# A two-block transformer step on one core: the unit-matrix products that fill TensorE's waits are left out

## What is computed

```
for l in range(2):                                   # first block
    mod = silu(c) @ w_ada[l] + b_ada[l]              # shift, scale, gate, twice
    h = rms_norm(x, norm1_g[l]) * (1 + scale1) + shift1
    proj = h @ w_in[l]
    mix = concat(mla_group(proj...), conv_group(proj...)) @ w_out[l]
    x = x + gate1 * mix
    h2 = rms_norm(x, norm2_g[l]) * (1 + scale2) + shift2
    x = x + gate2 * expert_choice_ffn(h2, w_router[l], w_gate[l], w_up[l], w_down[l])
xn = rms_norm(x, mix_norm_w)                         # second block
q, f, i, g, lru_x, lru_gate = split(xn @ w_in_2)
x = x + concat(hgrn2_mix(q, f, i, g), rglru_mix(lru_x, lru_gate)) @ w_out_2
x = x + (silu(gate) * up) @ w_down_2                 # gate, up = split(rms_norm(x) @ w_gate_up)
out = rms_norm(x)
```

## Time and profile before

| | us |
|---|---|
| median of 3 runs | 3365.02 |
| lowest, highest | 3361.22, 3365.70 |
| profiled execution, device time | 3364.91 |
| its span, first to last instruction | 3363.1 |
| outside the span | 1.8 |

### The profile page before, as it was taken

How to read it: one execution, slowest core, us unless ns; L and a number is a source line. 1 busy time by engine, 2 the same in 40 slices (tenths; PEclk the granted TensorE clock), 3 DMA queues, 4 the chain that set the end, 5 groups by cost and what they waited for, 6 DMA issues and landing times. The chain is left out here.

```text
span 3363.1 us, 43670 instructions
## 1 busy us (share of the span) xinstructions
PE 3237.5 (96%) x15480; PEld 2605.3 (77%) x15480; DVE 2704.8 (80%) x2483; ACT 1784.7 (53%) x1912; POOL 685.3 (20%) x550
## 2 busy tenths in 40 slices
PE   7999997999999999999799999999999999999998
PEld 4859884888888786897588888878777878888786
DVE  7988886888888798888788888886744488888767
ACT  4254534888888534444378888863333353333223
POOL 0212100111111020320011111104453023233233
PEclk9999998999999999999899999999999999999999
DMA  5130167999999412005599999962110434444953
GB/s 200 38 97 13 33 211 281 398 400 389 400 389 399 172 46 90 21 10 177 193 363 391 402 388 403 391 255 98 47 38 13 150 107 162 138 156 148 379 238 137
DMA packets 143518, 703.07 MB, mean 209 GB/s; under 512 B 19376, under 2 KB 28080, under 8 KB 90672
## 3 DMA queue, kind: packets, MB, share of 16 engines
q1 hardware_dynamic: 132240, 664.65, 51.4%
q0 software_dynamic: 8928, 32.51, 3.6%
q10 hardware_dynamic: 2240, 4.46, 0.3%
HBM read 608.75 MB, written 85.46 MB: 206 GB/s over the span
## 5 line engine op out<-in xcount | busy, mean ns | idle before, releaser
L2226 DVE TENSOR_TENSOR ex_lo_layer<-mix_layer,ex_hi_layer 128x2048 fp32r<-128x2048 f32 x128 | 291.7, 2290 | 22.9 <-ACT ex_hi_layer L2157 21.2
L2226 DVE TENSOR_TENSOR ex_lo<-mix,ex_hi 128x2048 fp32r<-128x2048 f32 x128 | 291.6, 2289 | 22.4 <-ACT ex_hi L2157 21.1
L2157 ACT CAST ex_hi_layer<-mix_layer 128x2048 fp32r<-128x2048 f32 x126 | 240.8, 1912 | 64.9 <-PE psum L2075 50.8
L2157 ACT CAST ex_hi<-mix 128x2048 fp32r<-128x2048 f32 x126 | 240.8, 1912 | 52.1 <-PE psum L2075 50.7
L3199 PE MATMUL psum<-ff_rest,w_hi 128*128 128x512 f32 x776 | 239.8, 390 | 8.2 <-DVE ff_ev L3477 4.0
L2073 PE MATMUL psum<-ex_hi_layer,xe_hi_layer 128*128 128x512 f32 x512 | 200.8, 392 | 1.0 <-DVE xe_lo_layer L2231 1.0
L2073 PE MATMUL psum<-ex_hi,xe_hi 128*128 128x512 f32 x512 | 200.8, 392 | 1.0 <-DVE xe_lo L2231 1.0
L2075 PE MATMUL psum<-ex_hi_layer,xe_lo_layer 128*128 128x512 f32 x512 | 199.4, 389 | 0.0
L2075 PE MATMUL psum<-ex_hi,xe_lo 128*128 128x512 f32 x512 | 199.4, 389 | 0.0
L2074 PE MATMUL psum<-ex_lo,xe_hi 128*128 128x512 f32 x512 | 199.2, 389 | 0.0
L2074 PE MATMUL psum<-ex_lo_layer,xe_hi_layer 128*128 128x512 f32 x512 | 199.2, 389 | 0.0
(11 more groups left out here) (775 smaller groups left out, 8842.6 us busy)
## 6 DMA issues: line engine op xcount, KB each, us to landing
mix<-w_experts_dram SPq DMA_DIRECT2D x128, 1024.0 KB, 7.6
mix_layer<-w_experts_dram SPq DMA_DIRECT2D x128, 1024.0 KB, 7.1
first_w<-w_experts_dram SPq DMA_DIRECT2D x64, 1024.0 KB, 8.2
hid_rows<-x SPq DMA_DIRECT2D x71, 512.0 KB, 3.8
ex_raw<-w_experts_dram SPq DMA_DIRECT2D x32, 1024.0 KB, 7.8
ex_raw_layer<-w_experts_dram SPq DMA_DIRECT2D x32, 1024.0 KB, 7.6
first_w<-w_in_dram SPq DMA_DIRECT2D x42, 512.0 KB, 3.2
ff_rest<-hid_rows SPq DMA_DIRECT2D x13, 1536.0 KB, 13.5
```

The lines of the kernel that those rows point to most:

```text
L2157: act.copy(hi[j % PARTS][:], raw[j % RAW][:]).then_inc(w_hi, 1)
L2226: dve.tensor_tensor(lo[j % PARTS][:], raw[j % RAW][:], hi[j % PARTS][:].bitcast(F32), ALU.subtract).then_inc(w_lo, 1)
```

## The change

Every call of `keep_busy` is left out, in fourteen places of the text, and the helper with them. No other instruction, wait or buffer is touched.

```diff
@@ helper
-        def keep_busy(pe, out, count):
-
-            for _ in range(count):
-                pe.matmul(psum[:, out, 0:HALF // 2], ident, const[:, 0:HALF // 2], start=True, stop=True)
@@ setup, end
                         mm.then_inc(turned, 1)
-                        keep_busy(pe, 7, 1)
@@ project, start
-                        keep_busy(pe, 7, 6 if l else 3)
                         for b in range(2):
                             pe.sem_inc(done[b], 1)
@@ heads, end
                         squares(n_k + 6)
-                        keep_busy(pe, 0, 3)
                         turn_roots(1)
-                        keep_busy(pe, 0, 5)
@@ attend, start
                         scores(0, 0, 0)
                         scores(1, 1, 0)
-                        keep_busy(pe, 7, 6)
@@ attend, end
                         for h in range(2, HEADS):
                             outputs(h, h % 2, g + h, last_blk)
-                        keep_busy(pe, 4, 4)
@@ conv_norm_and_mix, start
-                        keep_busy(pe, 7, 4)
                         for n in range(LO_BUFS):
@@ route, end
-                        if not n_rows:
-                            keep_busy(pe, 1, 2)
@@ run_experts, start and end
-                        keep_busy(pe, 6, 10)
                         turn_rows(0)
...
-                        keep_busy(pe, 0, 6)
@@ project2, start
-                        keep_busy(pe, 7, 5)
@@ mixers, end
                         row_of_sums(TB - 1)
-                        keep_busy(pe, ke_bank, 3)
```

## The result

The changed kernel takes 3379.04 us (median of 5, 3377.24 to 3382.13) against 3365.02: ratio 1.004, 95% interval 1.0029 to 1.0051, that is 10 to 17 us slower. The forecast was 3381, slower. The profiled execution took 3380.67 us with a span of 3378.9, 15.8 over the span of before.

The account below looks back on a forecast made before the run. TensorE, busy for 96% of the span, was taken to set the kernel's length. Clock-dip losses of 20.7 us less 4.2 gained at boundaries gave 16.5 over 3364.91, so 3381 us, range 3370 to 3393.

Parts of the forecast that it names:

- The clock falls behind every empty stretch of 3.5 us or more: At block boundaries left without fillers: a dip to clock 0.50 behind each, about 2.3 us lost for one dip.
- the forecast's 3 in 10: In attend: chance of a second dip behind the 2.6 us wait, 1.7 us lost each time, counted as 0.5.
- `attend`: nothing takes the loss off: Heads to attend: first scores run in the dip and everything follows them; 2.8 us lost each, 5.6 in two layers.
- `run_experts`: Start of run_experts: 2.3 us lost in dense products and 0.6 in first-row transposes; 2.9 each, 5.8 in two layers.
- `conv_norm_and_mix`: 2.3 less 0.2 of waits: Start of conv_norm_and_mix: a dip's 2.3 us less 0.2 taken by later waits, 4.2 lost in two layers.
- `project`: slack of 1.5: Start of project: a wait for ACT absorbs 1.5 us of a dip's loss, leaving 0.3 in layer 0, 0.8 in layer 1.
- `project2` and feed-forward: Their starts: project2 loses 2.3 less a 0.6 wait for DVE, 1.7 us; feed-forward loses 2.3, with nothing taken off.
- The gains: Boundaries come earlier: attend's end 2.8 us in two layers, run_experts' end 0.9, route's end 0.5; 4.2 in all.
- the first (slack takes the dips): Every empty stretch: clock needs no fillers or slack takes the dips; only gains remain, 3360.7 us, not slower; chance 0.11.
- the third (transposes): In attend: transposes don't hold the clock up, half clock for a third of it, 27 us lost twice, 3435; chance 0.03.
- the fourth: Block boundaries: more fillers on the path than those found, so faster by more than 6.7 us; chance 0.02.
- the second (dips 6 us longer): In attend and run_experts: dips 6 us longer, 3 us more lost in four places, 3395 in all; chance 0.12.

Follow-up runs that it names:

- e9: Kernel of before without the filler products at the start of project2, end of mixers and start of the feed-forward part: 3373.15 us against 3365.09, ratio 1.002.
- e4: Kernel of before without only the 6 filler products behind the first scores in attend, both layers: 3369.21 us against 3364.05, ratio 1.0008.
- e3: Kernel of before without the 8 filler products at the end of heads and the 6 in attend, both layers: 3371.89 us against 3366.6, ratio 1.0022.
- e2: Kernel of before without only the 10 filler products at the start of run_experts, both layers: 3372.03 us against 3366.6, ratio 1.0019.
- e7: Kernel of before without the filler products at the end of setup, start of project and end of run_experts in layer 0: 3368.96 us against 3364.05, ratio 1.0011.
- e1: Kernel of before, fillers cut at the ends of attend, run_experts and route, 7 for 4 at conv_norm_and_mix's start: 3362.48 us against 3366.6, ratio 0.9987.
- e8: Kernel of before, block-end fillers cut, those around project left out, new ones at route's start and project2's end: 3359.35 us against 3364.05, ratio 0.9982.
- e5: Kernel of before with each filler product replaced by four transposes of the unit matrix: 3369.32 us against 3366.6, ratio 1.0008.
- e10: Kernel of before without the 4 filler products at attend's end and the 4 at conv_norm_and_mix's start, both layers: 3366.92 us against 3365.09, ratio 1.0004.
- e11: Kernel of before without only the 3 and 6 filler products at the start of project: 3367.39 us against 3365.09, ratio 1.001.
- e6: Kernel of before with each filler product of 256 columns replaced by two of one column: 3386.22 us against 3364.05, ratio 1.0062.

## Why the prediction was right

The verdict, the size (16.5 forecast, 14.0 and 15.5 measured) and the mechanism hold. By its steps:

- **The clock falls behind every empty stretch of 3.5 us or more.** Right at all ten places in the profiled execution, though not a rule: e9 has 3.65 us without a dip. Behind the 2.6 us in `attend` it fell in one layer of two where a dip stands at the start, and in both layers of e4, where none does: the forecast's 3 in 10 was too low. Its list of waits in the trace of before left out two kinds: the clock had fallen there behind 1.94 and 2.38 us as well, each with a wait of 0.3 beside it, and had stayed up behind 2.60 us and 3.04. The forecast came through this unharmed because nearly all of its places are longer than 3.5 us.
- **A dip lasts 4.6 us into dense work.** The nine dips of the changed kernel behind first products, but for the first `project`, last 3.45 to 6.06 us, mean 4.4.
- **Half of it is lost where TensorE is waited for.** In e3 layer 1 has one dip, of 5.2 us into the stage, and loses 2.44; layer 0 has two, 6.8 us in all, and loses 3.14. In e2 2.39 and 2.32 us are lost.
- **`attend`: nothing takes the loss off.** Right: 3.2 and 2.3 against 2.8 each.
- **`run_experts`.** Right: 3.3 (2.35 and the 0.9 gained at its end) and 2.4 against 2.9 each.
- **`conv_norm_and_mix`: 2.3 less 0.2 of waits.** Mis-sized. The dips of 5.9 and 4.5 us would lose 2.9 and 2.2; the stage grew by 1.95 and 1.29. About 1 us of the loss is taken up there, not 0.2. The 0.2 is what TensorE's products sit idle in the first 7 us, but its weight loads sit idle for longer there, and the products start later by more than the idle time says (0.44 and 0.57 us apart in place of 0.23). The loads of before:

```profile
416.81 0.30 PEld L497 LDWEIGHTS psum<-lo_mix_hi,lo_hi 128*128 128x128 f32 x2 [0.48 <-DVE lo_mix_lo L1557]
421.35 0.30 PEld L497 LDWEIGHTS psum<-lo_mix_hi,lo_hi 128*128 128x128 f32 x2 [0.60 <-DVE lo_lo L1563]
```

  Counted by the starts of the products, these two waits are worth 0.8 us, and in the changed kernel both are gone.
- **`project`: slack of 1.5.** Mis-sized: the two terms were 1.1, the profiled execution shows 0.2. The slack is two waits and not one, 2.0 us in all. First the one for the low part, of before and of the changed kernel, layer 1:

```profile
1163.22 0.74 PE L792 MATMUL psum<-h_lo_layer,in_hi_layer 128*128 128x512 f32 x2 [1.09 <-DVE h_lo_layer L718]
```

```profile
1170.31 1.22 PE L787 MATMUL psum<-h_lo_layer,in_hi_layer 128*128 128x512 f32 x2 [0.21 <-DVE h_lo_layer L713]
```

  Then the one that the forecast had:

```profile
1193.31 0.70 PE L492 MATMUL psum<-h_hi_layer,in_hi_layer 128*128 128x512 f32 x2 [1.25 <-ACT mix_layer L665]
```

  It starts 25.25 us behind the first product at 1168.06, against 25.26 in the earlier trace rows, with a dip in one and none in the other. Of the loss the first wait gave 0.88 us and the second, 1.25 in place of 1.62, the other 0.37. The second goes down to 0.5 and no lower in any profile, so it is worth 1.1; the first gives its 0.9 only to a dip that has begun before it. The dip of before and e4's began too late for it. This fits that e7's dips, 5.3 and 4.7 us into the stage, cost nothing and e4's of 6.8, begun 1.6 us into it, cost 1.28 more; no run was made for it alone.
- **`project2` and feed-forward.** Each too high by 0.7 to 0.9: 0.8 against 1.7, 1.6 (107.71 against 106.10 to the wait near 2716) against 2.3. Both dips were short ones, 3.68 and 3.45 us. Half of that is 1.7 in the feed-forward part, so there only the dip's length was off; in `project2` the stage took up 1.0 of 1.8, where the forecast had 0.6.
- **The gains.** 2.8 at the end of `attend` (e1: 1.41 and 1.43) and 0.9 at the end of `run_experts` (e7: 0.93, e8: 0.96) are right to a tenth. The 0.5 at the end of `route` isn't seen apart: `route` is 0.8 to 1.1 us shorter than before in layer 1 in seven kernels that keep both products (e2, e3, e5, e7, e9, e10, e11), too, and in e1, which cuts one of them, it isn't shorter.
- **Net.** Losses by stage 16.9, gains 3.7, 13.2 in all, where the forecast had 16.5. The other 2.6 us of the profiled 15.8 are 1.2 ahead of the first `project`, 2.7 late in the last stage, 0.3 in `mixers`, and 1.6 less in `route`, of which the forecast had 0.5. The forecast's terms for the smaller places were somewhat high, by 3.8 us of losses in all, and these others, which but for the 0.3 no run ties to the fillers, made up for it. That the total came within 1 us of the profiled one is luck; the stages bear out 13.2.

Of the rivals, the first (slack takes the dips) is true of `project`, and of a third to somewhat over a half of the loss in `conv_norm_and_mix` and `project2`; the third (transposes) is out by e5, and the fourth has nothing for it. Of the second (dips 6 us longer) nothing shows but the second dip in `attend`, which the forecast had at a part of its price.

## What to carry to other kernels

A filler product is priced by two rows: which engine reaches the next boundary last (TensorE must not), and how long the wait behind it would be empty. Fillers behind a boundary, as long as the wait and no longer, cost nothing and kept the clock in most profiles here; the same fillers ahead of it delay everyone, and longer ones behind it delay the stage (e8). Where they end 1.3 us or more ahead of the next work and a second wait follows at once, the clock can fall in spite of them (e1, e5, e9 to e11). Where the first dense work is followed by waits for another engine, as in `project`, the dip is paid from those waits as far as they can shrink and no further; read them in the weight loads' rows as well as in the products'.

## What the runs showed of the hardware that was not expected

- With transposes as fillers the mean clock was 0.988, as with products of 256 columns; with products of one column it was 0.978, though TensorE shows an instruction at nearly every moment of the wait.
- The length of a wait alone doesn't tell whether the clock falls: it fell behind 1.86 and 1.05 us with 1.1 us of transposes between them (e1), and stayed up through 3.65 us (e9).
- Some stages repeat to 0.05 us from kernel to kernel where no dip falls into them (`heads` 56.87 to 56.92 in all kernels but e6), so that their length in one profile tells tenths of a microsecond, where a median of 11 whole executions tells 3 us. Not all do: `conv_norm_and_mix` of layer 0 took 105.93 in e5, without a dip, where before took 105.07.
- With the DMA engines' share at 1.0 the same stretch of work moved 412 GB/s in one execution and 350 in another.
